# Sums of two weight tiles made in DRAM by accumulating DMAs instead of on VectorE

## The chip, the cores and the metric

The kernel runs on one core of one Trainium2 chip. The metric is the device time of one launch in microseconds (us). Three runs of the kernel before took 1962.23, 1961.20 and 1960.32 us; their median is 1961.2 us.

## The reference, cut to what matters

The reference is a trunk of two layers on 512 + 256 tokens, each sequence with 16 learned tokens ahead of it, so 800 token columns in all (T). Layer 0 mixes with a bidirectional mLSTM, layer 1 with differential attention. Each mixer is followed by the same feed-forward part (FFN), and the change is in that part:

```python
def swiglu(xn, w_in, w_out):
    gu = xn @ w_in            # 1024 x 5632
    g = gu[..., :FF]          # "gate", FF = 2816 columns
    u = gu[..., FF:]          # "up"
    return (jax.nn.silu(g) * u) @ w_out
```

All inputs are float32. A residual stream `h` is added after each mixer and each FFN, and an RMS norm stands ahead of each.

## The kernel before, in words

**How a product is made.** Every float32 weight tile is cut in two: a high half rounded to the matmul's type (a copy on ScalarE or on GpSimd, `wh`, `wxh`) and the rest (a subtraction, `wl`, `wxl`). The activations are cut the same way, and TensorE does three of the four half products. Weights come by DMA on SyncE's queue into two staging slots, `raw`, and one spare piece, `rawx`.

**The FFN's first product** goes by tiles of 128 columns of FF: 22 tiles a layer, in groups of 4, 6, 6 and 6 (GROUPS). A tile g is a pair of column tiles, gate and up. Its products are done by a scheme with seven multiplications in place of eight (a Strassen-Winograd form with the two rows gate and up, and the even and the odd 128-row tiles of k as the other index). So tile g has four quarters of 128 x 512 elements, called `quad(row, col, g)`: row 0 gate, row 1 up, col 0 the even k tiles, col 1 the odd ones. The factors of the seven products (NPROD = 7) are: j=0 gate even, j=3 gate odd, j=6 up odd, and four sums of quarters that VectorE forms in place:

- `sum_1` (L1296 to L1300): up even + up odd, into up even's place. It is the factor j=1. It waits for the loads of both up quarters.
- `sum_2` (L1305): sum_1 less gate even, factor j=2; it waits for sum_1 and for the low half of j=0.
- `sum_3` (L1310): up odd less sum_2, factor j=4; it waits for the low half of j=1.
- `sum_4` (L1314): gate odd less sum_2, factor j=5.

ScalarE makes the high halves (`weight_high`, L2044) and waits for the sum or the load that a factor comes from; GpSimd makes the low halves (`split_product`, L571), seven a tile, in the order of j. At the first tile of a later group VectorE makes the low halves itself (`factor_low`, L1319). TensorE's seven products of a tile are `product` (L719). VectorE adds the products' results: `gate_first_half` (L1456), `up_second_half` (L1464), `gate_second_half` (L1470), `gate_scaled` (L1476), `up_first_half` (L1427), `hidden` (L1434, L1439), `hidden_low` (L1237). The seventh product of a tile waits for `up_second_half` of the same tile.

**The FFN's second product** (with w_out) follows each group: 8 blocks of TensorE work (`run_block`, L647), whose weights GpSimd cuts (L558, L562).

**The mixers** use the same block form: 24 blocks of 8 k tiles in the mLSTM (blocks 0 to 23, six a head) and 24 in the attention (MIX1 to MIX1+23). GpSimd cuts block n (`split`) once TensorE has finished block n-2, and SyncE loads block n once block n-2 has been cut, so that weights lie about two blocks ahead.

**What sets the order.** Each engine's program is written out by hand, in order, and semaphores stand between the engines. Two counters matter here: `wsum_ready`, raised by each sum (four a tile), and `prod_split`, raised by each low half. SyncE's FFN program loads up odd, gate even, up even and gate odd of tile g as their places come free.

Of the kernel before, what the change touches and what calls it, by code (L numbers as in the profile page):

```python
# [27 lines left out]
P = 128  # L28
# [12 lines left out]
FT = FF // P  # L41
GROUPS = (4, 6, 6, 6)
M_HEADS, M_DK, M_DV = 4, 128, 256
D_HEADS, D_HD = 8, 64
# [129 lines left out]
def trunk(nc, x_prompt, x_sample, meta_tokens, norm_mix, norm_ffn, m_w_in, m_b_gate, m_g_head, m_w_out,  # L174
# [3 lines left out]
    with ctx:  # L178
# [22 lines left out]
        def place(at, *tensors):  # L201

            with ExitStack() as stack:
                if at:
# [21 lines left out]
        vl_parts = [y[:, KT - 2:KT, :].rearrange("p a b -> p (a b)")[:, 0:len(tiles) * (M_DV + 2)]  # L226
                    .rearrange("p (i c) -> p i c", i=len(tiles)) for y, tiles in zip((yh, yl), OF_SEQ)]
        h_kept = nc.dram_tensor("h_kept", (P, KP, T), F32, kind="Internal").ap()
        mrow, = place(WK_AT + 9 * ROW, ("mrow", [P, T], F32))
# [168 lines left out]
        wsum_ready, prod_hi, prod_split, prod_done = sem("wsum_ready"), sem("prod_hi"), sem("prod_split"), sem("prod_done")  # L398
        squares_taken = sem("squares_taken")
        copy_ready, sum_ready, um_ready, g_ready = sem("copy_ready"), sem("sum_ready"), sem("um_ready"), sem("g_ready")  # L400
        xf_ready, tx_ready, sxh_ready, sxl_ready = sem("xf_ready"), sem("tx_ready"), sem("sxh_ready"), sem("sxl_ready")
# [18 lines left out]
        def _(sp):  # L420
# [23 lines left out]
            def load_quad(row, col, g, layer):  # L444
                f = g - layer * FT
                c = f * P + row * FF
                src = ffn_w_in[layer].rearrange("(k e p) n -> e p k n", e=2, p=P)[col][:, :, c:c + P]
                sp.dma_start(quad(row, col, g).rearrange("p (k c) -> p k c", k=KP), src)\
                  .then_inc(last_quad_in[g % 2] if row and col else quad_in[2 * row + col], 16)

            def ffn_blocks(layer):
                for gi, first, tiles, n0 in pair_groups(layer):
                    for g in range(first, first + tiles):
                        if g == first:
                            sp.wait_ge(w_split, n0 - 1)
                            load_quad(0, 0, g, layer)
                            load_quad(0, 1, g, layer)
                            sp.wait_ge(w_split, n0)
                            load_quad(1, 0, g, layer)
                            load_quad(1, 1, g, layer)  # L460
                            continue
                        if g == first + 1 and gi == 0:
                            sp.wait_ge(yl_ready, YL_AT[(FFN0, FFN1)[layer]])
                        else:
                            sp.wait_ge(prod_split, NPROD * (g - 1))
                        load_quad(1, 1, g, layer)
                        sp.wait_ge(wsum_ready, 4 * g)
                        sp.wait_ge(prod_split, NPROD * (g - 1) + 3)
                        load_quad(0, 0, g, layer)
                        sp.wait_ge(prod_split, NPROD * (g - 1) + 5)  # L470
                        load_quad(1, 0, g, layer)
                        sp.wait_ge(prod_split, NPROD * (g - 1) + 6)
                        load_quad(0, 1, g, layer)
# [59 lines left out]
        def _(pool):  # L533
# [57 lines left out]
            split(1, 1, 1, wait=False)  # L591
            with pool.Fori(1, FFN0 // 2) as i:
                for slot in range(2):
                    split(i * 2 + slot, slot, i + 1)
            ffn(0)
# [13 lines left out]

            with pool.Fori(MIX1 // 2, OUT1 // 2) as i:  # L610
                for slot in range(2):
                    split(i * 2 + slot, slot, i + 1)
            for q in range(4):
# [603 lines left out]
        def _(ve):  # L1217
# [77 lines left out]

            def sum_1(g):  # L1296
                row, col = quad(1, 0, g), quad(1, 1, g)
                ve.wait_ge(quad_in[2], 16 * (g + 1))
                ve.wait_ge(last_quad_in[g % 2], 16 * (g // 2 + 1))
                ve.tensor_tensor(row, row, col, ALU.add).then_inc(wsum_ready, 1)  # L1300

            def sum_2(g):
                ve.wait_ge(wsum_ready, 4 * g + 1)
                ve.wait_ge(prod_split, NPROD * g + 1)
                ve.tensor_tensor(quad(0, 0, g), quad(1, 0, g), quad(0, 0, g), ALU.subtract).then_inc(wsum_ready, 1)  # L1305

            def sum_3(g):
                ve.wait_ge(wsum_ready, 4 * g + 2)
                ve.wait_ge(prod_split, NPROD * g + 2)
                ve.tensor_tensor(quad(1, 0, g), quad(1, 1, g), quad(0, 0, g), ALU.subtract).then_inc(wsum_ready, 1)  # L1310
# [19 lines left out]
            def combinations(layer, at):  # L1330
# [21 lines left out]
                elif at == 0:  # L1352
                    add_tile(WHOLE1, LATE[0], 0)
                if last and layer == 0:
                    sum_1(g)
                ve.wait_ge(xf_ready, KT * layer + 2 * at + 1)
# [19 lines left out]
                if layer == 1 and at < 2:  # L1376
                    add_rest(at, *((2, 1), (0, 3))[at])
                    if at == 1:
                        sum_1(g)
                elif layer == 1 and at == 2:  # L1380
# [37 lines left out]
            def ffn(layer):  # L1418
# [59 lines left out]
                for gi, first, tiles, n0 in pair_groups(layer):  # L1478
                    for i in range(tiles):
                        g, more = first + i, i + 1 < tiles  # L1480
                        if g == f0:
                            gate_first_half(g)
                            up_second_half(g)
                            sum_1(g + 1)
                            sum_2(g + 1)
# [5 lines left out]
                        if g == f0 + 1:  # L1491
# [3 lines left out]
                            up_second_half(g)  # L1495
                            sum_1(g + 1)
                            sum_2(g + 1)
# [6 lines left out]
                        elif g == f0 + 2:  # L1504
# [4 lines left out]
                            up_second_half(g)  # L1509
                            sum_1(g + 1)  # L1510
                            sum_2(g + 1)
# [4 lines left out]
                        elif i == 0:  # L1516
                            sum_1(g + 1)
                            gate_first_half(g)
# [6 lines left out]
                        else:  # L1525
                            up_first_half(g - 1)
                            hidden(g - 1)
                            if more:
                                sum_1(g + 1)
                            hidden_low(g - 1, i - 1)  # L1530
# [18 lines left out]
                    for m in range(KT):  # L1549
# [11 lines left out]
                        if m == KT - 2 and not ends:  # L1561
                            sum_1(g)
                            factor_low(g, 0)
                            sum_2(g)
                            factor_low(g, 1)
                            sum_3(g)
# [433 lines left out]
        def _(sc):  # L2000
# [26 lines left out]
            def weight_high(g, j, n0, first):  # L2027
# [12 lines left out]
                elif j == 6:  # L2040
                    sc.wait_ge(last_quad_in[g % 2], 16 * (g // 2 + 1))
                else:
                    sc.wait_ge(wsum_ready, 4 * g + {1: 1, 2: 2, 4: 3, 5: 4}[j])
                sc.activation(slot_of(j, 0), factor(g, j), ACT.Copy).then_inc(prod_hi, 1)  # L2044
# [259 lines left out]
            root(1)  # L2304


            a = Steps(sc, astep)
            a(sc.activation(small[:, 3:4], epsc, ACT.Exp))
# [142 lines left out]
            def head(hd, odd, n, first=False, last=False):  # L2451
# [42 lines left out]
                if not first:  # L2494
                    deliver(hd - 1, 1)

            squares_of(wk[:, 2, :], k_sq, MIX1 + 1)
            squares_of(wk[:, 0, 0:TQ], q_sq, MIX1 + 2)
# [48 lines left out]
```

## Time and profile before

| What | Value |
|---|---|
| Median of three runs | 1961.2 us |
| Profiled execution, first to last instruction (span) | 1959.5 us |
| TensorE matmul (PE) busy | 1930.5 us, 99% |
| VectorE (DVE) busy | 1157.8 us, 59% |
| GpSimd (POOL) busy | 1021.9 us, 52% |
| ScalarE (ACT) busy | 721.8 us, 37% |
| DMA | 114.90 MB, mean 59 GB/s |
| TensorE clock granted | 1.000 of full speed |

The profile was taken of one execution; what its launch takes outside the span isn't in it, and the median of the runs is 1.7 us above its span. Stages by the time line: mLSTM up to about 382 us, its output product and FFN of layer 0 up to about 978 us, attention up to about 1405 us, FFN of layer 1 up to the end. PE is TensorE's matmul, PEld its weight load. A row of the time line gives start, duration, engine, line, operation, tiles, a count of instructions joined in the row, and in brackets how long the engine sat idle before it and who ended that.

### The profile page before, as it was taken

The page shows a single profiled execution, that of the slowest core. Times are in us where ns is not written, and L with a number is a line of the kernel's source. Part 1 is how long each engine was busy: PE and PEld are TensorE (multiplying, and loading weights), DVE is VectorE, ACT ScalarE, POOL GpSimd, SP SyncE. Part 2 cuts the span into 40 slices and gives each one's busy share as a digit, 9 for nine tenths or more (in the row PEclk, how much of TensorE's full clock was granted, in tenths as well). Part 3 has the DMA queues.
Part 4 walks back from the last instruction along what each step waited for, and adds up shares of the span by engine and source line. Part 5 has one row for each costly group of instructions (what it writes and reads, how often), then busy time and mean ns, then how long its engine had stood idle before and what let it go on. Part 6 is the DMA issues. An engine that isn't in the chain of part 4 may idle for free.

```text
span 1959.5 us, 30288 instructions
## 1 busy us (share of the span) xinstructions
PE 1930.5 (99%) x11145; PEld 1801.5 (92%) x11145; DVE 1157.8 (59%) x1966; ACT 721.8 (37%) x1448; POOL 1021.9 (52%) x1419
## 2 busy tenths in 40 slices
PE   7999999999999999999999999999999999999999
PEld 7898988999999999999988888888889998998998
DVE  7756464777465265265676666666575662662651
ACT  6333333445143143143234444445462340430431
POOL 4432323358487386396632222222557694683773
PEclk9999999999999999999999999999999999999999
DMA  4111101212221221222211111101211222222223
GB/s 160 43 33 37 50 23 42 77 48 60 70 85 51 72 74 54 76 65 71 68 43 33 33 33 32 32 27 38 60 44 56 85 65 68 73 71 60 77 58 97
DMA packets 214920, 114.90 MB, mean 59 GB/s; under 512 B 7011, under 2 KB 213510, under 8 KB 214550
## 3 DMA queue, kind: packets, MB, share of 16 engines
q1 hardware_dynamic: 212816, 112.62, 19.6%
q8 instruction: 73, 1.20, 0.3%
q10 hardware_dynamic: 1990, 0.76, 0.2%
q14 instruction: 41, 0.34, 0.1%
HBM read 108.57 MB, written 4.78 MB: 58 GB/s over the span
## 4 chain that ended last, share of the span: by engine, by line
PE 87%; DVE 5%; POOL 3%; ACT 2%; issue 1%; DMA 1%; ACTq 0%; DVEq 0%; SPq 0%; POOLq 0%
PE ps L647 44%; PE ps L719 29%; PE ps L909 3%; PE ps L1070 2%; PE ps L1038 2%; POOL wl L571 2%; PE ps L889 1%; PE ps L1060 1%; PE ps L972 1%; POOL wxl L571 1%; PE ps L918 1%; PE ps L1002 0%; DVE sx L1344 0%; DMA raw<-in_ffn_w_in_dram 0%; DVE h L1256 0%
## 5 line engine op out<-in xcount | busy, mean ns | idle before, releaser
L558 POOL CAST wh<-raw 128x256 fp32r<-128x256 f32 x428 | 168.4, 433 | 734.1 <-PE ps L647 695.3
L719 PE MATMUL ps<-sx,wh 128*128 128x400 f32 (+1 forms) x1408 | 366.6, 341 | 2.1 <-POOL wl L571 1.2
L571 POOL TENSOR_TENSOR wl<-raw,wh 128x256 fp32r<-128x256 f32 x304 | 275.8, 936 | 158.3 <-ACT wh L2044 158.2
L562 POOL TENSOR_TENSOR wl<-raw,wh 128x256 fp32r<-128x256 f32 x428 | 332.5, 806 | 10.4
L719 PE MATMUL ps<-sx,wxh 128*128 128x400 f32 (+1 forms) x1056 | 275.0, 341 | 5.1 <-DVE ut L1464 5.0
L719 PEld LDWEIGHTS ps<-sx,wh 128*128 128x128 f32 x1408 | 257.4, 188 | 3.6 <-ACT p L2051 2.2
L719 PE MATMUL ps<-sx,wl 128*128 128x400 f32 (+1 forms) x704 | 240.1, 341 | 0.0
L2044 ACT ACTIVATE wh<-raw 128x512 fp32r<-128x512 f32 x176 | 106.4, 626 | 354.0 <-PE ps L647 242.8
L647 PE MATMUL ps<-xh,wh 128*128 128x400 f32 (+2 forms) x768 | 221.3, 364 | 0.0
L647 PE MATMUL ps<-xl,wh 128*128 128x400 f32 (+2 forms) x768 | 212.9, 351 | 0.0
L647 PE MATMUL ps<-xh,wl 128*128 128x400 f32 (+2 forms) x768 | 206.8, 347 | 0.0
L571 POOL TENSOR_TENSOR wxl<-raw,wxh 128x256 fp32r<-128x256 f32 x184 | 194.6, 1082 | 12.0 <-ACT wxh L2044 12.0
L719 PEld LDWEIGHTS ps<-sx,wxh 128*128 128x128 f32 x1056 | 192.6, 188 | 7.7 <-DVE ut L1464 7.0
L647 PE MATMUL ps<-fyh,wh 128*128 128x400 f32 (+1 forms) x704 | 184.6, 342 | 1.3 <-DVE fyl L1237 0.6
L647 PE MATMUL ps<-fyl,wh 128*128 128x400 f32 (+1 forms) x704 | 184.1, 341 | 0.0
L647 PE MATMUL ps<-fyh,wl 128*128 128x400 f32 (+1 forms) x704 | 183.8, 340 | 0.0
L719 PE MATMUL ps<-sx,wxl 128*128 128x400 f32 (+1 forms) x528 | 179.3, 340 | 0.0
L647 PEld LDWEIGHTS ps<-xh,wh 128*128 128x128 f32 x768 | 131.0, 189 | 12.7 <-issue 7.4
L647 PEld LDWEIGHTS ps<-xl,wh 128*128 128x128 f32 x768 | 139.4, 188 | 2.4
L647 PEld LDWEIGHTS ps<-xh,wl 128*128 128x128 f32 x768 | 138.2, 188 | 2.4
L719 PEld LDWEIGHTS ps<-sx,wl 128*128 128x128 f32 x704 | 132.2, 188 | 0.0
L647 PEld LDWEIGHTS ps<-fyh,wh 128*128 128x128 f32 x704 | 119.5, 188 | 9.2 <-issue 1.3
(281 smaller groups left out, 3369.6 us busy)
## 6 DMA issues: line engine op xcount, KB each, us to landing
raw<-in_ffn_w_in_dram SPq DMA_DIRECT2D x154, 256.0 KB, 3.1
raw<-in_ffn_w_out_dram SPq DMA_DIRECT2D x48, 384.0 KB, 3.5
raw<-in_m_w_in_dram SPq DMA_DIRECT2D x24, 512.0 KB, 3.9
raw<-in_d_w_in_dram SPq DMA_DIRECT2D x24, 512.0 KB, 3.9
rawx<-in_ffn_w_in_dram SPq DMA_DIRECT2D x22, 256.0 KB, 3.2
raw<-in_m_w_out_dram SPq DMA_DIRECT2D x8, 512.0 KB, 4.2
raw<-in_ffn_w_out_dram SPq DMA_DIRECT2D x16, 256.0 KB, 2.8
wk<-in_x_prompt_dram SPq DMA_DIRECT2D x4, 512.0 KB, 5.9
```

What stands on the lines that cost most here:

```text
L558: ins = pool.tensor_copy(wh[:, slot, c], raw[:, slot, c])
L562: ins = pool.tensor_tensor(wl[:, slot, c], raw[:, slot, c], wh[:, slot, c].bitcast(F32), ALU.subtract)
L571: ins = pool.tensor_tensor(slot_of(j, 1)[:, c], factor(g, j)[:, c], slot_of(j, 0)[:, c].bitcast(F32), ALU.subtract)
L647: mm = pe.matmul(out, w[:, slot, k * P:(k + 1) * P], x[:, k, a:b], start=(k + q == 0), stop=(k == k_tiles - 1 and q == 2), skip_group_chec ...
L719: mm = pe.matmul(product_bank(g, j, layer), slot_of(j, low_w)[:, k * P:(k + 1) * P], sx[layer][:, k * NPROD + j, low_x, :], start=(j in OP ...
L889: mm = pe.matmul(flat(2 + 0)[0:tz, (j % 2) * 1024 + a:(j % 2) * 1024 + b], wk[:, 1, t0:t0 + tz], wk[:, 0, START[s] + a:START[s] + b], star ...
L909: mm = pe.matmul(ps[0:tz, 4 + 2 * (i % 2) + d, 0:M_DV + 2], w, v, start=(j == js[0] and t == 0), stop=(j == js[-1] and t == 2), skip_group ...
L918: mm = pe.transpose(flat(2)[:, c * 1024 + t0:c * 1024 + t0 + tz], hn(i)[0:tz, c * P:(c + 1) * P], ident[0:tz, 0:tz])
L972: mm = pe.matmul(square_sums[0:lhs.shape[1], 2 * i:2 * i + 2], lhs, cst[:, COMP:COMP + 2], start=True, stop=True, skip_group_check=True)
L1038: return pe.matmul(both[:, c, a:b], wk[rows, odd, i * P:(i + 1) * P], wk[rows, 2 + odd, START[s] + a:START[s] + b], start=True, stop=True)
L1070: mm = pe.matmul(acc_o, at[:, i % 2, q, :], va[:, odd, j, :], start=(q == 0), stop=(j == js[-1]), skip_group_check=True)
L2044: sc.activation(slot_of(j, 0), factor(g, j), ACT.Copy).then_inc(prod_hi, 1)
```

## The change

`sum_1` is gone from VectorE. In its place a DRAM tensor `up_sums[layer]` of 512 x 2816 float32 holds up even + up odd for all 22 tiles of a layer. It is made in two steps, in four column parts of 704 (UP_PARTS):

- ScalarE issues four plain DMAs that copy up's even k tiles from the weights into `up_sums` (`copy_up_even`): those for layer 0 after the first norm's root, ahead of the gate work of the mLSTM; those for layer 1 at the start of the attention.
- GpSimd waits for these copies and issues four DMAs that add up's odd k tiles (`add_up_odd`, `accum_op`): after cutting block 11 for layer 0, after cutting block MIX1+9 for layer 1. Its loop over blocks is cut in two there.

SyncE waits for the four sums of the layer before its first FFN load, and loads the quarter up even from `up_sums` (the same 128 x 512 elements, 512 B a row). ScalarE takes the high half of j=1 as soon as that load has landed. `sum_3` now has the wait for up odd's load that `sum_1` had, and `wsum_ready` counts three a tile.

```diff
+UP_PARTS = [slice(a, a + FF // 4) for a in range(0, FF, FF // 4)]
+        up_sums = [nc.dram_tensor(f"up_sums{layer}", (KP * P, FF), F32, kind="Internal").ap() for layer in range(2)]
@@ SyncE
-                src = ffn_w_in[layer].rearrange("(k e p) n -> e p k n", e=2, p=P)[col][:, :, c:c + P]
+                if row and not col:
+                    src = up_sums[layer].rearrange("(k p) n -> p k n", p=P)[:, :, f * P:(f + 1) * P]
+                else:
+                    src = ffn_w_in[layer].rearrange("(k e p) n -> e p k n", e=2, p=P)[col][:, :, c:c + P]
             def ffn_blocks(layer):
+                sp.wait_ge(up_sums_ready, 16 * len(UP_PARTS) * (layer + 1))
...
-                        sp.wait_ge(wsum_ready, 4 * g)
+                        sp.wait_ge(wsum_ready, 3 * g)
@@ GpSimd
+            def add_up_odd(layer):
+                up = ffn_w_in[layer].rearrange("(k e p) n -> e p k n", e=2, p=P)[1][:, :, FF:2 * FF]
+                pool.wait_ge(up_even_in, 16 * len(UP_PARTS) * (layer + 1))
+                for c in UP_PARTS:
+                    pool.dma_start(up_sums[layer].rearrange("(k p) n -> p k n", p=P)[:, :, c], up[:, :, c],
+                                   accum_op=ALU.add).then_inc(up_sums_ready, 16)
...
+            splits(1, 6)
+            add_up_odd(0)
+            splits(6, FFN0 // 2)
             ffn(0)
...
+            splits(MIX1 // 2, MIX1 // 2 + 5)
+            add_up_odd(1)
+            splits(MIX1 // 2 + 5, OUT1 // 2)
@@ VectorE
-            def sum_1(g):
-                row, col = quad(1, 0, g), quad(1, 1, g)
-                ve.wait_ge(quad_in[2], 16 * (g + 1))
-                ve.wait_ge(last_quad_in[g % 2], 16 * (g // 2 + 1))
-                ve.tensor_tensor(row, row, col, ALU.add).then_inc(wsum_ready, 1)
-
             def sum_2(g):
-                ve.wait_ge(wsum_ready, 4 * g + 1)
+                ve.wait_ge(quad_in[2], 16 * (g + 1))
...
             def sum_3(g):
-                ve.wait_ge(wsum_ready, 4 * g + 2)
+                ve.wait_ge(wsum_ready, 3 * g + 1)
+                ve.wait_ge(last_quad_in[g % 2], 16 * (g // 2 + 1))
...
(and all calls of sum_1)
@@ ScalarE
+                elif j == 1:
+                    sc.wait_ge(quad_in[2], 16 * (g + 1))
                 else:
-                    sc.wait_ge(wsum_ready, 4 * g + {1: 1, 2: 2, 4: 3, 5: 4}[j])
+                    sc.wait_ge(wsum_ready, 3 * g + {2: 1, 4: 2, 5: 3}[j])
...
+            def copy_up_even(layer):
+                up = ffn_w_in[layer].rearrange("(k e p) n -> e p k n", e=2, p=P)[0][:, :, FF:2 * FF]
+                for c in UP_PARTS:
+                    sc.dma_start(up_sums[layer].rearrange("(k p) n -> p k n", p=P)[:, :, c], up[:, :, c]).then_inc(up_even_in, 16)
+
+            copy_up_even(0)
             a = Steps(sc, astep)
             a(sc.activation(small[:, 3:4], epsc, ACT.Exp))
...
+            copy_up_even(1)
             squares_of(wk[:, 2, :], k_sq, MIX1 + 1)
```

VectorE, in the FFN of layer 1, at the first tile of the second group and the tile after it. Before, `sum_1` is L1300, ahead of the two halves that TensorE's results go through:

```order
L1300 TENSOR_TENSOR raw<-raw,rawx 128x512
L1456 TENSOR_TENSOR gt<-ps,p 128x384
L1464 TENSOR_TENSOR ut<-ps,p 128x384
L1305 TENSOR_TENSOR raw<-raw 128x512
L1310 TENSOR_TENSOR raw<-rawx,raw 128x512
L1470 TENSOR_TENSOR gt<-ps,u 128x384
L1476 TENSOR_TENSOR gt<-gt,rstd 128x768
L1314 TENSOR_TENSOR raw<-raw 128x512
L1427 TENSOR_TENSOR ut<-ps,rstd 128x384
L1434 TENSOR_TENSOR ut<-ut,rstd 128x384
L1439 TENSOR_TENSOR ut<-gt,ut 128x768
L1300 TENSOR_TENSOR raw<-raw 128x512
```

The same place now, where L1467 is `gate_first_half`, L1475 `up_second_half`, L1319 `sum_2`, L1325 `sum_3`, L1329 `sum_4` and L1257 `hidden_low`:

```order
L1467 TENSOR_TENSOR gt<-ps,p 128x384
L1475 TENSOR_TENSOR ut<-ps,p 128x384
L1319 TENSOR_TENSOR raw<-raw 128x512
L1325 TENSOR_TENSOR raw<-rawx,raw 128x512
L1481 TENSOR_TENSOR gt<-ps,u 128x384
L1487 TENSOR_TENSOR gt<-gt,rstd 128x768
L1329 TENSOR_TENSOR raw<-raw 128x512
L1438 TENSOR_TENSOR ut<-ps,rstd 128x384
L1445 TENSOR_TENSOR ut<-ut,rstd 128x384
L1450 TENSOR_TENSOR ut<-gt,ut 128x768
L1257 TENSOR_TENSOR fyl<-ut,fyh 128x768
```

The two instructions of `sum_1` are gone, and nothing else has changed its place among VectorE's instructions.

GpSimd, in the mLSTM, at the end of the first of its two loops over blocks (L565 and L569 are the cut of a block, L604 the accumulating DMAs, L608 the loop):

```order
L565 CAST wh<-raw 128x256 x4
L567 REGISTER_ALU
L569 TENSOR_TENSOR wl<-raw,wh 128x256 x4
L608 REGISTER_ALU
L608 COMPARE_AND_BRANCH
L604 DMA up_sums<-in_ffn_w_in_dram 128x4x704 x4
L608 UNCONDITIONAL_BRANCH
```

The four DMAs stand in GpSimd's own order, between the cut of block 11 and that of block 12; before, the loop ran through.

## Rows read from the trace of the kernel before

**Rows 1.** The page's first lines: span, and busy time of each engine.

```profile
span 1959.5 us, 30288 instructions
PE 1930.5 (99%) x11145; PEld 1801.5 (92%) x11145; DVE 1157.8 (59%) x1966; ACT 721.8 (37%) x1448; POOL 1021.9 (52%) x1419
```

**Rows 2.** Waits of TensorE: waiting line, who ended it, total us, times, longest.

```profile
PE ps L802 <- DMA wk<-in_x_prompt_dram: 6.2, 1, 6.2
PE ps L719 <- DVE ut L1464: 5.0, 6, 2.0
```

**Rows 3.** Time line of TensorE, FFN of layer 1, and one of layer 0.

```profile
562.79 0.63 PE L719 MATMUL ps<-sx,wxh 128*128 128x400 f32 x2 [0.44 <-DVE ut L1464]
...
1435.55 0.62 PE L719 MATMUL ps<-sx,wh 128*128 128x384 f32 x2 [0.61 <-DVE sx L1344]
...
1440.08 0.58 PE L719 MATMUL ps<-sx,wh 128*128 128x384 f32 x2 [1.21 <-POOL wl L571]
...
1560.62 0.62 PE L719 MATMUL ps<-sx,wxh 128*128 128x384 f32 x2 [1.99 <-DVE ut L1464]
...
1700.29 0.61 PE L719 MATMUL ps<-sx,wxh 128*128 128x384 f32 x2 [1.03 <-DVE ut L1464]
...
1839.60 0.62 PE L719 MATMUL ps<-sx,wxh 128*128 128x384 f32 x2 [0.70 <-DVE ut L1464]
```

**Rows 4.** sum_1 in the view of its line, L1300: durations min/median/max in ns.

```profile
L1300 DVE TENSOR_TENSOR raw<-raw x22: 681/740/1246, 427.6 to 1860.7; 128x512 f32<-128x512 f32 x22
L1300 DVE TENSOR_TENSOR raw<-raw,rawx x22: 692/1109/1237, 447.1 to 1875.2; 128x512 f32<-128x512 f32 x22
```

**Rows 5.** Time line of VectorE, FFN of layer 1: its start, and second group.

```profile
1420.24 0.75 DVE L1300 TENSOR_TENSOR raw<-raw 128x512 f32<-128x512 f32 x1
...
1541.12 0.69 DVE L1300 TENSOR_TENSOR raw<-raw,rawx 128x512 f32<-128x512 f32 x1 [3.30 <-DMA raw<-in_ffn_w_in_dram]
...
1693.96 0.69 DVE L1300 TENSOR_TENSOR raw<-raw 128x512 f32<-128x512 f32 x1 [2.33 <-DMA raw<-in_ffn_w_in_dram]
```

**Rows 6.** Time line of ScalarE and GpSimd in the FFN.

```profile
1541.91 0.63 ACT L2044 ACTIVATE wh<-raw 128x512 fp32r<-128x512 f32 x1 [2.33 <-DVE raw L1300]
...
556.94 4.04 POOL L571 TENSOR_TENSOR wl<-raw,wh 128x256 fp32r<-128x256 f32 x4 [0.77 <-ACT wh L2044]
...
1542.62 1.88 POOL L571 TENSOR_TENSOR wl<-raw,wh 128x256 fp32r<-128x256 f32 x2 [1.46 <-ACT wh L2044]
...
1554.40 4.44 POOL L571 TENSOR_TENSOR wl<-raw,wh 128x256 fp32r<-128x256 f32 x4
...
1819.06 2.90 POOL L571 TENSOR_TENSOR wl<-raw,wh 128x256 fp32r<-128x256 f32 x4 [16.49 <-ACT wh L2044]
```

**Rows 7.** Time line of ScalarE at the start of the mLSTM.

```profile
43.00 0.97 ACT L2310 ACTIVATE wk<-wk,par 128x800 f32<-128x800 f32 x1 [4.73 <-DVE wk L1635]
```

**Rows 8.** DMA issues (KB each, median us to landing); then SyncE's time line.

```profile
raw<-in_m_w_in_dram SPq DMA_DIRECT2D x24, 512.0 KB, 3.9
...
h_kept<-h SPq DMA_DIRECT2D x1, 1600.0 KB, 7.6
...
4.05 3.06 SPq L487 DMA_DIRECT2D wk<-in_x_sample_dram  x2
...
414.60 9.65 SPq L448 DMA_DIRECT2D raw<-in_ffn_w_in_dram  x4
```

**Rows 9.** Time line of GpSimd in the two mixers.

```profile
55.82 4.07 POOL L558 CAST wh<-raw 128x256 fp32r<-128x256 f32 x4 [1.11 <-PE ps L647]
...
167.77 2.01 POOL L558 CAST wh<-raw 128x256 fp32r<-128x256 f32 x4 [11.59 <-PE ps L647]
...
189.24 1.44 POOL L558 CAST wh<-raw 128x256 fp32r<-128x256 f32 x4 [16.57 <-PE ps L647]
...
1099.09 1.43 POOL L558 CAST wh<-raw 128x256 fp32r<-128x256 f32 x4 [14.63 <-PE ps L647]
...
1111.61 1.44 POOL L558 CAST wh<-raw 128x256 fp32r<-128x256 f32 x4 [7.84 <-PE ps L647]
```

More of the change, by code:

```diff
@@ L399, in trunk @@
         squares_taken = sem("squares_taken")
+        up_even_in, up_sums_ready = sem("up_even_in"), sem("up_sums_ready")
         copy_ready, sum_ready, um_ready, g_ready = sem("copy_ready"), sem("sum_ready"), sem("um_ready"), sem("g_ready")
@@ L591, in _, with splits @@
             split(1, 1, 1, wait=False)
-            with pool.Fori(1, FFN0 // 2) as i:
-                for slot in range(2):
-                    split(i * 2 + slot, slot, i + 1)
+            def add_up_odd(layer):
[4 more added lines that the diff above has]
+                                   accum_op=ALU.add).then_inc(up_sums_ready, 16)
+            def splits(first, last):
+                with pool.Fori(first, last) as i:
+                    for slot in range(2):
+                        split(i * 2 + slot, slot, i + 1)
+            splits(1, 6)
+            add_up_odd(0)
+            splits(6, FFN0 // 2)
             ffn(0)
@@ L608, in split_rest @@
                 ins.then_inc(w_split, 1)
-            with pool.Fori(MIX1 // 2, OUT1 // 2) as i:
-                for slot in range(2):
-                    split(i * 2 + slot, slot, i + 1)
+            splits(MIX1 // 2, MIX1 // 2 + 5)
+            add_up_odd(1)
+            splits(MIX1 // 2 + 5, OUT1 // 2)
             for q in range(4):
@@ L1294, in out_blocks, with sum_2 @@
                 invert(norm + 1)
-            def sum_1(g):
-                row, col = quad(1, 0, g), quad(1, 1, g)
+            def sum_2(g):
                 ve.wait_ge(quad_in[2], 16 * (g + 1))
-                ve.wait_ge(last_quad_in[g % 2], 16 * (g // 2 + 1))
-                ve.tensor_tensor(row, row, col, ALU.add).then_inc(wsum_ready, 1)
-            def sum_2(g):
-                ve.wait_ge(wsum_ready, 4 * g + 1)
                 ve.wait_ge(prod_split, NPROD * g + 1)
@@ L1353, in combinations @@
                     add_tile(WHOLE1, LATE[0], 0)
-                if last and layer == 0:
-                    sum_1(g)
                 ve.wait_ge(xf_ready, KT * layer + 2 * at + 1)
@@ L1377, in combinations @@
                     add_rest(at, *((2, 1), (0, 3))[at])
-                    if at == 1:
-                        sum_1(g)
                 elif layer == 1 and at == 2:
@@ L1483, in ffn @@
                             up_second_half(g)
-                            sum_1(g + 1)
                             sum_2(g + 1)
@@ L1495, in ffn @@
                             up_second_half(g)
-                            sum_1(g + 1)
                             sum_2(g + 1)
@@ L1509, in ffn @@
                             up_second_half(g)
-                            sum_1(g + 1)
                             sum_2(g + 1)
@@ L1516, in ffn @@
                         elif i == 0:
-                            sum_1(g + 1)
                             gate_first_half(g)
@@ L1527, in ffn @@
                             hidden(g - 1)
-                            if more:
-                                sum_1(g + 1)
                             hidden_low(g - 1, i - 1)
@@ L1561, in ffn @@
                         if m == KT - 2 and not ends:
-                            sum_1(g)
                             factor_low(g, 0)
```

## The prediction

> **What bounds the kernel now.** I read the page's busy times first: TensorE is busy 1930.5 of 1959.5 us [rows 1], so its idle time over the whole span is 29.0 us, and that is all that a change which leaves its matmuls alone can win. Next its waits: 6.2 us are the first load [rows 2], and the only large one in the FFN is 5.0 us, six waits for `up_second_half` (L1464) [rows 2]. The time line of TensorE shows where they lie: 0.44 us in layer 0 (one of three alike, at 562.79, 707.89 and 853.00), then 1.99, 1.03 and 0.70 us in layer 1, each at the second tile of a later group [rows 3]. At the start of layer 1's FFN TensorE waits further, 0.61 us for a low half of the activations and 1.21 us for GpSimd [rows 3]. Elsewhere in the FFN it hardly waits. So VectorE's 44 sums, however long, cost time only where they stand in the chains that end in these waits. How the 1.99 us come about is seen by going back from 1560.62: GpSimd works from 1544.70 on with next to no pause and reaches the low half of the next tile's j=1 late; `sum_3` needs that low half, and `up_second_half` stands behind `sum_3`.
>
> **What goes.** Twenty-two sums have a median of 740 ns and twenty-two of 1109 ns [rows 4], 41 us of VectorE in all by these medians; VectorE is 59% busy [rows 1], so nearly all of that lies beside TensorE's work. Four places count:
>
> - Start of layer 1: the sum at 1420.24 takes 0.75 us [rows 5], in the middle of the combinations that TensorE waits for from 1435 on. VectorE starts the next instruction 0.7 us earlier; what follows is a chain of VectorE and ScalarE without long pauses. I take 0.7 us won; the bounds are 0 (another link is late) and 1.8 us (the two waits of 0.61 and 1.21 us whole).
> - Second group of layer 1: the sum waits 3.30 us for the loads and ends at 1541.81 [rows 5]; ScalarE's high half of j=1 follows at 1541.91, GpSimd's low half at 1542.62, after 1.46 us of idle time [rows 6]. Now the high half can start when the load has landed, 0.7 us earlier; but `sum_2` still comes behind `up_second_half`, which waits for TensorE, so GpSimd's later work gains about 0.4 us. To it comes that the four low pieces from 1554.40 take 4.44 us [rows 6], 1.11 each, where four pieces with no VectorE sum beside them took 2.90 us, 0.73 each [rows 6]: one of the VectorE instructions beside them is a sum that goes, which I count 0.3 us. Together 0.7 us of the 1.99; bounds 0 and 1.99.
> - Third group of layer 1: the sum at 1693.96 [rows 5] lies beside the same four pieces, 0.3 us of the 1.03; bounds 0 and 1.03.
> - Last group of layer 1 and the three waits of layer 0: here GpSimd starts the pieces after a wait for ScalarE's high half of j=0 (556.94, 0.77 us [rows 6]), which itself follows a TensorE product; the sum is over by then. I take 0; bounds 0 and 0.70 + 3 x 0.44 = 2.0 us.
>
> Sum: 0.7 + 0.7 + 0.3 = 1.7 us, between 0 and 1.8 + 2.0 + 1.0 + 2.0 = 6.8 us.
>
> **What comes, and what hides it.**
>
> - ScalarE issues four copies before the gate work, and four at the start of the attention. In layer 0 it sits idle 4.73 us just there [rows 7]. SyncE's issues take some 0.5 us; the worst pair, two with a queue full of work behind it, took 3.06 us [rows 8]. Four are therefore 2 to 4.5 us: inside the gap, cost 0. Behind it are queued the gate exponentials, and VectorE's scans wait for them.
> - The copies move 512 rows of 2816 bytes a part, 5.77 MB read and as much written a layer. SyncE's loads of mixer blocks run beside them. A load lands in 3.9 us [rows 8], two blocks ahead. The tight one is block 4: issued at 42.6 us behind the 1600 KB store, which takes 7.6 us [rows 8], and needed for the cut at 55.82 [rows 9]. It has 55.8 - 42.6 - 3.9 = 9.3 us to spare. Cost 0 if the copies take half of the engines' time; if all 5.77 MB came first at the store's pace of 1600 KB in 7.6 us, 27 us, it would be some 18 us. The nearest row is the store ahead of that very load, with which it now shares its 9.3 us: I take 0.
> - GpSimd issues four accumulating DMAs a layer; the trace shows none, so the hold is bounded: below by SyncE's issues, 4 x 0.5 = 2 us; above by their landing, each at three times the store's traffic (two reads and a write), 4 x 7.6 x 3 x 1408/1600 = 80 us. Behind them stands the cut of block 12. Before it GpSimd idles 11.59 us, and after it 16.57 us until TensorE has finished block 11 [rows 9]: 28 us before TensorE feels it. In layer 1 the idle times are 14.63 and 7.84 us [rows 9], 22 us. I take the lower end, as it is an issue and not a wait for landing: 2 us, cost 0.
> - SyncE's new wait: the sums are issued where GpSimd's idle times begin, at 167.77 - 11.59 = 156 us and 1099.09 - 14.63 = 1084 us [rows 9], the first FFN loads at 414.60 [rows 8] and at about 1405 us. By the 80 us above, there are over 170 us to spare. The loads from `up_sums` have the same shape as before: 0.
>
> The Trainium skill, page "DMA: Bandwidth & Descriptors", section "Queues, rings and completion order", says that each DMA engine goes round the queues that have work and changes only at packet ends. By that block 4's load gets its share and the 18 us fall away; no row before has two queues with bulk work, so nothing here shows it. Against the change speaks the page "SBUF — State Buffer", section "Who interferes with whom": some VectorE instructions keep GpSimd from writing the descriptors of DMAs that it issues. By that the hold would stretch, which makes the second rival below likelier; the trace has no such DMA.
>
> **The sum.** 1959.5 - 1.7 + 0 = 1957.8 us of span. The median of the runs lies 1.7 us above the span, so 1961.2 - 1.7 = 1959.5 us. What a measurement of this kernel can tell from no change is about 0.2%, 3.9 us: this is no change.
>
> **Rivals.**
>
> 1. The waits vanish whole. The chains of rows 3 all pass through GpSimd, and the sum is one of their first links. All 6.8 us go: 1954.4 us. Against it: in layer 0 and in layer 1's last group GpSimd's start hangs on TensorE's own product, not on a sum.
> 2. GpSimd is held by its four DMAs (slower). Place: before the cut of block 12 and of block MIX1+10. It decides from 28 and 22 us, that is 7 and 5.6 us a DMA; at 10 us a DMA TensorE stands for 12 + 18 = 30 us: 1989.5 us; at 7.5 us a DMA 2 + 8 = 10 us: 1969.5 us. For it: the hold is unmeasured, with 80 us as its upper end. Against it: issues on other engines are about 0.5 us.
> 3. The copies get in the way at 37 us: ScalarE's issue blocks past its 4.73 us, or block 4's load is late by more than its 9.3 us and GpSimd's slack. Price up to 18 us; at a middle value of 8 us, 1967.5 us. Against it: only layer 0's start is tight.
> 4. The change does nothing that can be seen: the chains hang on loads and on TensorE, and the place of `sum_1` is taken by the wait for the load, 3.30 us at 1541.12 [rows 5]. 1961.2 us.
>
> **How the numbers follow.** Forecast 0.48, rival 1 0.14, rival 2 0.18, rival 3 0.10, rival 4 0.10. The first and the fourth are within 0.2%, as both lie less than 3.9 us off; rival 1 is faster, rivals 2 and 3 are slower. So faster 0.14, same 0.58, slower 0.28. The range goes down to 1955, which takes in part of rival 1, and up to 1972, which takes in the milder half of rivals 2 and 3 and leaves about 0.15 above. The likeliest case alone would be 1957.5 to 1961.5.
>
> **What the profile after would show.** Right: no L1300; at the second group of layer 1 GpSimd's j=1 starts under 1 us after j=0 with TensorE's wait near 1.3 us there; TensorE's idle time 1 to 3 us less; its waits in the mixers as before; ScalarE's four issues over in less than 4.7 us, and GpSimd's four in less than 20 us. The 1.03 and 0.70 us waits tell the share of GpSimd's slower pieces: if both stay, that 0.3 us was wrong. Wrong: a wait of TensorE for GpSimd's cut near 190 or 1112 us (rival 2), for a gate or block near 62 to 70 us (rival 3), or SyncE still waiting for sums at 415 us.

## The result and the profile after

The changed kernel takes 1967.8 us (median of 5 runs, 1966.1 to 1968.7), the kernel before 1961.2 in the runs beside it: ratio 1.0030, 95% interval 1.0019 to 1.0041. It is slower by 6.6 us, where 1959.5 and no change were forecast. The third rival, the copies in the way at 37 us, had named the place and 1967.5 us, with a chance of 0.10.

The head of the page after, to be held against [rows 1]:

```profile
span 1965.8 us, 30220 instructions
PE 1934.3 (98%) x11145; PEld 1805.7 (92%) x11145; DVE 1108.7 (56%) x1922; ACT 721.0 (37%) x1448; POOL 1009.6 (51%) x1427
```

VectorE has lost 49 us of work, and the span has grown by 6.3. The waits of TensorE after (who ended them: total us, times, longest) show why:

```profile
PE ps L667 <- POOL wl L569: 6.5, 2, 6.3
PE ps L822 <- DMA wk<-in_x_prompt_dram: 5.8, 1, 5.8
PE ps L739 <- DVE ut L1475: 4.2, 6, 1.4
```

The second and third answer to [rows 2]: the FFN's waits fell from 5.0 to 4.2 us. The first is new: GpSimd's split of a weight block. The time lines of SyncE and GpSimd after, from 37 us on (the bracket is the idle time before a row and what ended it), name the block:

```profile
37.32 0.37 SPq L426 DMA_DIRECT2D raw<-in_m_w_in_dram  x1
```

```profile
53.55 4.13 POOL L565 CAST wh<-raw 128x256 fp32r<-128x256 f32 x4 [10.82 <-DMA raw<-in_m_w_in_dram]
57.76 4.14 POOL L569 TENSOR_TENSOR wl<-raw,wh 128x256 fp32r<-128x256 f32 x4
62.62 1.43 POOL L565 CAST wh<-raw 128x256 fp32r<-128x256 f32 x4 [0.71 <-DMA raw<-in_m_w_in_dram]
```

The load issued at 37.32 is block 3's. The DMA view gives its size in KB and its time to landing in us, without the copies (before), and then beside them (after):

```profile
raw<-in_m_w_in_dram SPq DMA_DIRECT2D x1, 512.0 KB, 4.3
```

```profile
raw<-in_m_w_in_dram SPq DMA_DIRECT2D x1, 512.0 KB, 16.1
```

Before, block 3's split began at 46.96, 5.5 us after the load had landed, and waited for TensorE:

```profile
46.96 2.19 POOL L558 CAST wh<-raw 128x256 fp32r<-128x256 f32 x4 [4.37 <-PE ps L647]
```

After, the load lands at 53.4 and the split begins at 53.55, 6.6 us late. Block 4's load, issued behind it and behind the store of h, takes 19.7 us and lands at 62.46: its split waits for it too, at 62.62. TensorE's time line after:

```profile
55.18 0.53 PE L667 MATMUL ps<-xh,wl 128*128 128x400 f32 x2
61.96 1.03 PE L667 MATMUL ps<-xh,wh 128*128 128x400 f32 x2 [6.25 <-POOL wl L569]
62.79 0.87 PE L667 MATMUL ps<-xl,wh 128*128 128x400 f32 x2
...
65.46 0.75 PE L667 MATMUL ps<-xh,wl 128*128 128x400 f32 x2
66.04 0.53 PE L667 MATMUL ps<-xh,wh 128*128 128x400 f32 x2
```

It stands for 6.25 us, and then pairs of matmuls take 0.87 us where they took 0.53. The view by stretches (us, busy time and count of PE, PEld, DVE, ACT and POOL, granted clock, DMA share, GB/s), the same two stretches of before and then of after, and after's second stretch in halves, shows that the granted clock fell:

```profile
50.00:62.00 12.00, 12.00 (x67) 11.82 (x65) 11.67 (x12) 1.22 (x2) 10.81 (x10) 1.00 0.16 44
62.00:70.00 8.00, 8.00 (x51) 6.87 (x51) 3.65 (x9) 2.57 (x5) 5.35 (x11) 1.00 0.24 68
```

```profile
50.00:62.00 12.00, 5.75 (x33) 5.41 (x31) 11.21 (x12) 1.74 (x2) 8.28 (x8) 0.88 0.95 367
62.00:70.00 8.00, 8.00 (x34) 7.97 (x35) 0.00 (x0) 0.00 (x0) 4.22 (x8) 0.76 0.44 126
62.00:66.00 4.00, 4.00 (x12) 3.97 (x13) 0.00 (x0) 0.00 (x0) 3.30 (x7) 0.51 0.47 132
66.00:70.00 4.00, 4.00 (x23) 4.00 (x23) 0.00 (x0) 0.00 (x0) 0.92 (x2) 1.00 0.42 120
```

The 0.76 is a time at 0.5 (1.2 GHz in place of 2.4) up to about 66 us and a time at 1.0 behind it; the clock fell while TensorE stood. Both traces have 11145 matmuls, so they can be paired by number, and each has a lag. The matmul that began at 45.7 us before is 0.15 us late and the one at 64.3 is 8.44 late: 8.3 us, of which 6.25 are the wait and 2.0 the clock. From there the lag falls to 5.7 us at 1565 us and is 6.25 at the end: the FFNs do gain, some 2.2 us.

### The profile page after: what moved, and what is told of

Same layout as the page of the kernel before. It is cut to its first block, busy times and chain, and to the rows that moved or that the text cites. A ratio compares the mean times of both kernels' runs of the same rounds, so it can differ in the third digit from the quotient of the medians.

```text
span 1965.8 us, 30220 instructions
## 1 busy us (share of the span) xinstructions
PE 1934.3 (98%) x11145; PEld 1805.7 (92%) x11145; DVE 1108.7 (56%) x1922; ACT 721.0 (37%) x1448; POOL 1009.6 (51%) x1427
## 4 chain that ended last, share of the span: by engine, by line
PE 88%; DVE 5%; POOL 2%; ACT 2%; DMA 2%; issue 1%; ACTq 0%; DVEq 0%; POOLq 0%
PE ps L667 43%; PE ps L739 31%; PE ps L929 3%; PE ps L1090 2%; PE ps L1058 2%; POOL wl L578 2%; PE ps L909 1%; PE ps L1080 1%; DMA raw<-in_m_w_in_dram 1%; PE ps L992 1%; PE ps L938 1%; POOL wl L569 0%; DVE sx L1359 0%; PE ps L1022 0%; PE ps L894 0%
## 5 line engine op out<-in xcount | busy, mean ns | idle before, releaser
L565 POOL CAST wh<-raw 128x256 fp32r<-128x256 f32 x428 | 165.4, 426 | 744.9 <-PE ps L667 695.9
L578 POOL TENSOR_TENSOR wl<-raw,wh 128x256 fp32r<-128x256 f32 x304 | 270.0, 917 | 160.7 <-ACT wh L2050 160.5
L569 POOL TENSOR_TENSOR wl<-raw,wh 128x256 fp32r<-128x256 f32 x428 | 327.9, 795 | 10.3
L578 POOL TENSOR_TENSOR wxl<-raw,wxh 128x256 fp32r<-128x256 f32 x184 | 187.1, 1040 | 16.8 <-ACT wxh L2050 16.8
## 6 DMA issues: line engine op xcount, KB each, us to landing
up_sums<-in_ffn_w_in_dram POOLq DMA_DIRECT2D x8, 1408.0 KB, 22.7
```

The lines of the kernel that those rows point to most:

```text
L565: ins = pool.tensor_copy(wh[:, slot, c], raw[:, slot, c])
L569: ins = pool.tensor_tensor(wl[:, slot, c], raw[:, slot, c], wh[:, slot, c].bitcast(F32), ALU.subtract)
L578: ins = pool.tensor_tensor(slot_of(j, 1)[:, c], factor(g, j)[:, c], slot_of(j, 0)[:, c].bitcast(F32), ALU.subtract)
```

## The experiments

Three theories were open: A, the copies make the load late and nothing else costs; B, the loss lies in the accumulating DMAs or in the loads of the ready sums; C, any place for the copies hurts, by ScalarE's issues. A fourth question came up on the way: how a copy and a load share the DMA engines (in the expectations to it, and to the last run, the letters B and C stand for rivals of their own).

**One part alone: the copies.** The kernel before, with layer 0's copies issued where the change puts them, and read by nobody (GpSimd waits for their landing before the FFN).

```diff
+            copy_up_even(0)
             a = Steps(sc, astep)
```

> The kernel before with one part of the change alone: ScalarE issues layer 0's four copies at 36 us as the changed kernel does, but nothing reads them; there are no accumulating DMAs, no copies for layer 1, and VectorE makes all four sums of each tile as before. Theory A (the copies make the load of w_in's block 3 late): block 3's split starts near 53.5 us in place of 46.96, TensorE waits about 6.3 us for it near 62 us, its granted clock is 0.5 for some 7 us after that, which costs about 2 more, and none of the FFN's gain is there: 1961.2 + 8.3 = 1969.5 us (1968.5 to 1970.5). Rival B (the loss is in the accumulating DMAs or in the FFN's loads from the new tensor): no wait near 62 us, 1961.2 us (1960.3 to 1962).

Measured: 1970.2 us (1968.7 to 1971.0), ratio 1.0039 (1.0026 to 1.0053), 8.7 us more than the 1961.5 beside it. Its waits of TensorE:

```profile
PE ps L651 <- POOL wl L565: 6.2, 2, 5.9
```

Theory A's number, and B falls: the whole loss is there with no accumulating DMA and with no load of a sum from DRAM. By pairing the matmuls it is 8.6 us, 5.9 of them the wait and 2.7 the lower clock.

**The copies elsewhere.** The changed kernel with layer 0's copies behind the first head's state weights.

```diff
-            copy_up_even(0)
             a = Steps(sc, astep)
...
                 for j in OF_SEQ[0]:
                     state_weights_high(j)
+                if first:
+                    copy_up_even(0)
```

> The changed kernel with layer 0's four copies moved from 36 us to ScalarE's program place after the first head's state weights (near 85 us, where ScalarE was idle for 5.43 us before); everything else as changed. Theory A: block loads in flight there have 30 us and more until GpSimd splits them (the one issued at 88.5 is split at 119.5), so no wait comes in place of the one at 62 us, the clock stays at 1.0 and the gain in the FFNs is left alone: 1967.8 - 8.3 = 1959.5 us (1958.8 to 1960.2). Rival B (the loss is elsewhere): 1966 us or more. Rival C (the copies hurt wherever they are, by what they do to ScalarE's 4.5 us of issues or to GpSimd's splits): a wait of TensorE of 3 us or more between 85 and 125 us, 1963 us or more.

Measured: 1959.1 us (11 runs, 1958.3 to 1960.1), ratio 0.9986 (0.9977 to 0.9995). The copies went out at 84.4 us. The one block load beside them, issued at 88.8, took 15.2 us and landed at 104.0, and its split came at 119.8: no wait of TensorE for a split near 62 or between 85 and 125 us, clock 1.00. C falls, and this version beats both kernels, the kernel before by 2.4 us.

> The kernel with the copies at 85 us once more, beside the last one and the kernel before on the same chip: 1959.1 us, 0.12% below the kernel before, with no wait near 62 us.

The same kernel once more: 1959.5 us against 1961.7, ratio 0.9987 (0.9978 to 0.9996).

**Just 9 us later.** The copies behind ScalarE's third gate activation.

```diff
-            copy_up_even(0)
             a = Steps(sc, astep)
...
+            copy_up_even(0)
             sc.wait_ge(gate_m, 1)
```

> The changed kernel with layer 0's four copies issued some 11 us later, behind the third gate activation of ScalarE (near 47 us), when block 3's load (41.5) and block 4's (47.0) have landed or nearly so. Theory A by the time that each load has to spare: block 3 and 4 are in time, and the next victim is block 5's load, issued at 54.7 and split at 66.3; with the 16 to 20 us that loads took beside the copies it lands at 70 to 73, TensorE waits 4 to 7 us between 66 and 80 us and some clock is lost: 1963.5 to 1968.5 us, point 1966. A rival in which the harm is tied to 36 us (the store of h that is also in flight, or the loads queued just then): 1959.5 us.

Measured: 1959.4 us (1958.3 to 1960.1), ratio 0.9987 (0.9978 to 0.9996): a miss by 6.6 us. The copies went out at 44.9, not 47, so that half of their bytes were through when block 5's load was issued at 54.7. It took 11.9 us, not 16 to 20, and its split began half a microsecond late:

```profile
66.76 1.43 POOL L565 CAST wh<-raw 128x256 fp32r<-128x256 f32 x4 [3.06 <-DMA raw<-in_m_w_in_dram]
```

TensorE did not feel it. The number that came is the rival's, 1959.5: harm tied to 36 us. Against that rival speaks that loads beside the copies were slow here too, and at 85 us. So the account left is the lateness of a load against its own due time; but that a late load costs TensorE anywhere else than at 36 us no run shows, since this one was on the edge.

**Dose: two copies, then one, at 36 us**, the others at 85 us.

```diff
-            copy_up_even(0)
+            copy_up_even(0, UP_PARTS[:2])
...
+                if first:
+                    copy_up_even(0, UP_PARTS[2:])
```

> The changed kernel with two of layer 0's four copies left at 36 us and two moved to near 85 us. Theory A (block 3's load has 5.5 us to spare and the copies that were queued before it share the DMA engines with it): with half the bytes it lands near 46 to 48.5 us in place of 53.4, so 0 to 1.5 us too late: 1959.5 to 1961.5 us, point 1960.5, and less clock lost. A rival in which the price is proportional to the bytes copied at 36 us: half of 8.3 over 1959.5, 1963.6 us. A rival in which the first copy already puts the whole queue behind it: 1967.8 us.

> The changed kernel with one of layer 0's four copies left at 36 us and three moved to near 85 us. Block 3's load is split at 46.96 in the kernel before; with two copies in front it landed at 49.91 (12 us), with four at 53.4 (16 us). Theory A (only a load that lands after its split is due costs anything): one copy is over near 43 us, so the load lands near 45 us, in time: 1959.2 us, with no wait near 62 us. Rival (a price by bytes from the first one on; half the bytes cost 5.6 us, all 8.7): 2.8 us, 1962 us.

Measured: with two 1964.7 us (1963.2 to 1967.2), ratio 1.0013 (1.0004 to 1.0023); with one 1959.8 us (1957.9 to 1961.0), ratio 0.9984 (0.9975 to 0.9994). GpSimd's split of block 3 with two and with one:

```profile
50.05 3.84 POOL L565 CAST wh<-raw 128x256 fp32r<-128x256 f32 x4 [6.72 <-DMA raw<-in_m_w_in_dram]
```

```profile
47.06 2.19 POOL L565 CAST wh<-raw 128x256 fp32r<-128x256 f32 x4 [4.38 <-PE ps L667]
```

With one, the load takes 7.2 us and GpSimd still waits for TensorE, not for the load: no cost. With two it takes 12.0, its split begins 2.3 us late (the traces are 0.75 us apart there), and TensorE stands for 3.4 us. There theory A's number (1960.5) was wrong and the proportional rival's (1963.6) nearer, but the run with one copy (1959.8 for the rival's 1962) shows a threshold. A had missed three things. The load landed at 49.9 us, not at 46 to 48.5. The split itself, both steps, took 9.6 us (50.05 to 59.69) where it took 7.75 before. And the clock fell: pairing matmuls, this kernel loses 6.3 us between 46 and 64 us, 3.4 by the wait and 2.9 at the lower clock, more than the 2.0 that the wait of 6.25 cost on top.

**Row length of the copies.** Same bytes, same place; rows of 704 bytes (eight DMAs), and rows of 11264 (four DMAs).

```diff
-                for c in UP_PARTS:
-                    sc.dma_start(up_sums[layer].rearrange("(k p) n -> p k n", p=P)[:, :, c], up[:, :, c]).then_inc(up_even_in, 16)
+                cut = dict(i=2, w=FF // 16)
+                for k in range(KP):
+                    for i in range(2):
+                        sc.dma_start(up_sums[layer][k * P:(k + 1) * P].rearrange("p (j i w) -> i p j w", **cut)[i],
+                                     up[:, k, :].rearrange("p (j i w) -> i p j w", **cut)[i]).then_inc(up_even_in, 16)
```

```diff
+                for k in range(KP):
+                    sc.dma_start(up_sums[layer].rearrange("(k p) n -> p k n", p=P)[:, k, :], up[:, k, :]).then_inc(up_even_in, 16)
```

> The changed kernel with its copies where they were (36 us) and the same bytes, but cut into rows of 704 bytes in place of 2816: eight DMAs a layer, each every other 704-byte piece of one k tile, so eight issues of ScalarE in place of four. Theory A (each DMA engine takes one packet of the loads' queue and one of the copies' in turn, so the load of 1024 packets of 512 bytes, 64 on each of 16 engines, waits for 64 copy packets on each): a copy packet of 704 bytes takes about a quarter of the 0.128 us that one of 2816 took (76.6% of 16 engines over 22 us by 2112 packets), so block 3's load lands some 64 x 0.035 = 2.2 us later than alone, near 44 us: in time, no wait near 62 us; 1959.2 us, up to 1960 for the four issues more. Rival B (the copies and the load share the bytes per second, whatever their packets): the load lands near 53 us as with the changed kernel, 1967.8 us.

> The changed kernel with its copies where they were and the same bytes and the same four issues a layer, but each copy is one whole k tile, so its rows have 11264 bytes in place of 2816 (512 rows a layer, 32 on each engine). Theory A (turns by packets): if a row goes as one packet of some 0.5 us, the load's 64 packets on an engine get through only as the 32 rows run out, so block 3's load lands near 57 us in place of 53.4 and TensorE's wait grows by 3 to 6 us: 1971 to 1975 us. If long rows are cut into shorter packets, less, 1967.8 to 1971. Rival B (shares by bytes): as the changed kernel, 1967.8 us.

Measured: 704 bytes 1988.2 us (1987.0 to 1989.2), ratio 1.013 (1.0113 to 1.0147); 11264 bytes 1969.8 us, ratio 1.0034 (1.0022 to 1.0047; seven runs, of which one, at 4796 us, stays unexplained and isn't in the ratio). Block 3's load to landing, with rows of 704 and then of 11264 bytes:

```profile
raw<-in_m_w_in_dram SPq DMA_DIRECT2D x1, 512.0 KB, 7.9
```

```profile
raw<-in_m_w_in_dram SPq DMA_DIRECT2D x1, 512.0 KB, 21.8
```

7.9, 16.1 (2816 bytes) and 21.8 us, while the DMA engines moved 363, 358 and 326 GB/s from 38.5 or 39 us until shortly before the landing: the load does not get a share of the bytes, its share hangs on how long the other queue's rows are. The view of DMA queues shows how (packets, MB, share; q10 the copies, q1 SyncE's queue, here the load). All but a few packets of this view (16, 20 and 48 of under 512 bytes) are one row each. First rows of 704 bytes (41 to 44 us), then of 2816 (the changed kernel, 42 to 50 us), then of 11264 (41 to 55 us):

```profile
q10 hardware_dynamic: 835, 0.58, 61.6%
q1 hardware_dynamic: 835, 0.43, 48.3%
```

```profile
q10 hardware_dynamic: 782, 2.15, 81.4%
q1 hardware_dynamic: 775, 0.40, 19.7%
```

```profile
q10 hardware_dynamic: 406, 4.03, 92.3%
q1 hardware_dynamic: 398, 0.20, 6.9%
```

While both queues have work, they go all but row for row: by their bytes some 820, 760 and 360 rows of the copies to 835, 775 and 398 of the load. In the changed kernel a copy's row took some 0.14 us of an engine (81.4% of 16 engines over 8 us by 760 rows), so the load's 1024 rows, 64 an engine, stand behind some 8.7 us of copies. Most of the rest of the 11.8 us lost is a late start, which theory A did not have: none of the load's rows moved before 41.2 us, 3.9 us after its issue, where alone the first moved within 1.1 us. With rows of 704 too the first came 3.5 us after the issue, 2.4 later than alone: that is the larger part of the 3.6 us lost there, and theory A's 2.2 us of turns were only some 1.1. With rows of 11264 the turns alone would have taken some 37 us (64 rows of 0.58 us by that view, an estimate): the load landed at 58.8 because the copies ran out (the last landed at 58.0). That landing is near theory A's 57, but the time is below its 1971: TensorE's wait grew by 2.0 us to 8.3 and not by 3 to 6, as GpSimd's split took 4.7 us there and 8.35 in the changed kernel. Rival B, shares of the bytes, falls: the load landed at 45.0 and at 58.8, where by bytes it would have been near 53 both times.

With rows of 704 the load was in time, as theory A said, and the time was wrong by 29 us. ScalarE's time line shows a cost in the other branch of the third rival:

```profile
35.70 22.09 ACTq L2317 DMA_DIRECT2D up_sums<-in_ffn_w_in_dram  x8
57.82 1.28 ACT L2322 ACT_TABLE_LOAD   x1 [21.19 <-issue]
```

```profile
75.39 3.04 PE L878 MATMUL ps<-wk,ones 32*128 32x400 f32 x8 [13.37 <-DVE wk L1678]
```

Eight issues took 22.1 us, the fifth alone 7.8, where four issues of rows of 2816 took 3.16: the gate activations queued behind them came 16 us late (59.2 in place of 43.15), and TensorE stood for VectorE's gates for 13.4 us. In layer 1 the same eight issues lost another 12.3 us, by the pairing of matmuls. Theory A's mechanism held for the load, and its number fell by what the issues cost.

**VectorE's time given back.** The kernel with the copies at 85 us, with VectorE kept as busy as before (1156.9 us against 1157.8 before and 1110.3 without these instructions).

```diff
+            def sum_1(g):
+                col = quad(1, 1, g)
+                ve.wait_ge(quad_in[2], 16 * (g + 1))
+                ve.wait_ge(last_quad_in[g % 2], 16 * (g // 2 + 1))
+                ve.tensor_tensor(col, col, col, ALU.max).then_inc(idle_done, 1)
...
+                            sum_1(g + 1)
...
-                    sc.wait_ge(last_quad_in[g % 2], 16 * (g // 2 + 1))
+                    sc.wait_ge(idle_done, g + 1)
```

> The kernel with the copies at 85 us, to which VectorE gets 44 instructions of the old sums' size back, in the old places: each takes the maximum of the odd quarter with itself (the same 512 columns, two loads' waits, values unchanged), and ScalarE's high half of that odd quarter waits for it; the sums themselves still come ready from DRAM, so the high half of j=1 starts as soon as its load has landed. It parts the gain of 2.1 to 2.4 us into VectorE's time and the earlier data. Theory A (the prediction's split: at the start of layer 1 all from VectorE's time; at the second group about 0.4 from the earlier high half, the rest from VectorE): about 1 us is lost at the start of layer 1 and 0.3 to 0.8 at the second group: 1960.4 us. Rival B (all of it is VectorE's time): 1961.3 us, as the kernel before. Rival C (all of it is the earlier data): 1959.1 us.

Measured: 1960.2 us (1959.7 to 1962.4), ratio 0.9993 (0.9984 to 1.0002), between the 1959.5 without these instructions and the 1961.7 of before. The intervals overlap; the time lines of TensorE part it better. The second tile of layer 1's second and third group, with VectorE free (copies at 85 us), then with it kept busy; before, [rows 3], 1.99 and 1.03:

```profile
1558.65 0.62 PE L739 MATMUL ps<-sx,wxh 128*128 128x384 f32 x2 [0.72 <-DVE ut L1475]
...
1698.17 0.61 PE L739 MATMUL ps<-sx,wxh 128*128 128x384 f32 x2 [0.90 <-DVE ut L1475]
```

```profile
1433.39 1.56 PE L693 MATMUL ps<-sq_late,ones 128*128 128x512 f32 x4 [0.34 <-ACT sq_late L2127]
...
1559.27 0.61 PE L740 MATMUL ps<-sx,wxh 128*128 128x384 f32 x2 [0.98 <-DVE ut L1486]
...
1699.08 0.62 PE L740 MATMUL ps<-sx,wxh 128*128 128x384 f32 x2 [1.20 <-DVE ut L1486]
```

Of the 1.27 us at the second group, 1.01 stay when VectorE is busy: they come from the earlier data. At layer 1's start the wait at 1433, 0 with VectorE free, is back at 0.34; pairing the matmuls from 1397 to 1510 us, 0.36 of the 1.0 us won there are left, so 0.65 were VectorE's time. Nearly all of it lies at that one wait: with VectorE free 0.60 us are won there, with VectorE busy none.

## Why the prediction was wrong, step by step

- **The step that failed: "The tight one is block 4 ... I take 0."** Two things in it. First, the wrong load: block 3's, issued 5.45 us earlier, had 46.96 - 41.48 = 5.5 us to spare, less than block 4's 9.3. It had no term in the sum; every load from 36 us on needed one, with issue, landing and due time. Second, the size: "if the copies take half of the engines' time" a load of 4.3 us takes some 9 and block 4 is in time. Block 3's took 16.1: it started 2.9 us later than alone and then went all but row for row with copies whose rows are 5.5 times as long as its own (2816 bytes to 512). Block 4's took 19.7 us, 15.3 more than the 4.4 it took before: it too was late by more than its 9.3. What TensorE paid for block 3's was 6.25 us of wait and 2.0 at the lower clock.
- **The rule that was weighed.** The Trainium skill, page "DMA: Bandwidth & Descriptors", section "Queues, rings and completion order", says that an engine goes round its queues at packet ends. The traces agree: at three row lengths the two queues' packets went all but one for one (835 to 835, 782 to 775, 406 to 398). The prediction drew the wrong end from it: it let 18 us "fall away", but did not ask how long a turn of the other queue is.
- **The third rival's price** of 8 us was a middle value. That it came out near the measured 8.3 is luck: it hangs on ScalarE's issues or block 4's load and has no clock, and the 8.3 are 6.25 us of wait for block 3 and 2.0 at half the clock. The prediction priced no wait with its clock.
- **What can be told from no change.** The prediction put it at 0.2%, 3.9 us. The intervals of these runs are some 0.1% to either side, so the loss of 6.6 us and the gain of 2.4 us both stand clear of no change.
- **ScalarE's four issues, 2 to 4.5 us inside 4.73 of idle time: right.** They took 3.16 us, and 2.48 us of idle time were left (ScalarE's time line after, below). Eight issues of shorter rows show that this step was nearer to an edge than it looked.

```profile
35.98 3.16 ACTq L2315 DMA_DIRECT2D up_sums<-in_ffn_w_in_dram  x4
...
43.15 0.97 ACT L2321 ACTIVATE wk<-wk,par 128x800 f32<-128x800 f32 x1 [2.48 <-DVE wk L1639]
```

- **GpSimd's four DMAs, held 2 us: right in effect.** They took 5.2 and 5.5 us, no stretched hold and well short of the 28 and 22 us at hand (GpSimd's time line after, layer 0 below), and landed after 12 to 34 us. The second rival, with 0.18 the largest, has nothing for it in any run: in its place, block 12's split, GpSimd still waits for TensorE.

```profile
164.53 5.19 POOL L604 DMA_DIRECT2D up_sums<-in_ffn_w_in_dram  x4
176.20 1.99 POOL L565 CAST wh<-raw 128x256 fp32r<-128x256 f32 x4 [6.48 <-PE ps L667]
```

- **SyncE's wait for the sums: right.** They were complete at 199.8 and 1128.8 us, over 200 us before they are loaded.
- **The gain, 1.7 us: near in size, partly by luck, and only partly in place.** In the four runs with the copies out of the way it is 2.1 to 2.4 us by the medians. By the traces: at layer 1's start 1.0 us (0.7 forecast), but the two waits on which that rested, 0.61 and 1.21 us [rows 3], stayed at 0.60 and 1.20; smaller ones of 0.35 (1433 us, ahead of them), 0.33 and 0.53 us went, and one of 0.83 came. At the second group 1.27 us (0.7 forecast): 0.26 go with VectorE's time (0.3 forecast) and 1.01 with the earlier data (0.4 forecast). The prediction let the high half of j=1 start 0.7 us earlier; with the copies at 85 us it starts 0.81 us after that of j=0 (1537.71 and 1538.52), where it started 2.96 us after it before, as the load that it hangs on lands at 1538.44 and not at 1541.10. At the third nothing that stands out (0.3 forecast): 0.13 and 0.01 in the two runs with the copies at 85 us, -0.35 with the changed kernel itself, -0.46 to 0.31 in the others. So terms that were too small and one that did not come made up a sum near the right one. The last group and layer 0's second tiles, forecast at 0, are as they were: 0.72 us for 0.70, and 0.47 for 0.44.

So the change gains about what the forecast said in the FFNs, and pays 8.3 us at 62 us for where its copies start. What stays open: why an issue blocks as it does behind some thousands of rows, and why the load's first row moves 2.4 to 2.9 us later beside the copies, whatever the length of their rows.

## What to carry to other kernels

Before bulk transfers are put on a second queue, list every load in flight beside them with its landing and its due time, take the smallest difference, and put one row of the other queue ahead of each row of the load rather than halving its speed: here that made some 8.7 us, and a late start 2.9. A wait that this makes on TensorE costs its own length and here 2.0 to 2.9 us more at the lower clock. Where a load was needed only 31 us after its issue, the same bytes cost nothing, and neither did a quarter of them at the tight place.

## What the runs showed of the hardware that was not expected

- A copy from DRAM to DRAM on another queue made a load of 512 KB take 7.9, 16.1 or 21.8 us in place of 4.3, with rows of 704, 2816 or 11264 bytes, at 363, 358 and 326 GB/s in all. The two queues went all but row for row at each length.
- Eight issues of 1024 rows each held ScalarE for 22.1 us (15.7 us in layer 1), four of 512 rows for 3.2.
- A stop of TensorE of 3.4 us cost 2.9 us more at a granted clock of 0.5, one of 6.25 us cost 2.0 more, and one of 8.3 us (rows of 11264 bytes) 2.0: the clock's price did not grow with the wait.
- Accumulating DMAs of 1408 KB landed after a median of 22.7 us, and GpSimd was free of all four after 5.2 and 5.5 us.
